# Expert matrices stored by partition, and the index of a job's rows loaded one job ahead

## The reference, cut to what matters

```python
N_EXPERTS = 32; TOP_K = 2; D_MODEL = 1024; EXPERT_HIDDEN = 512
order = jnp.argsort(flat_e)                     # flat_e: two experts per token
tok = order // TOP_K
xs = h[tok]
a = lax.ragged_dot(xs, w_gate, sizes)           # w_gate, w_up: (32, 1024, 512)
u = lax.ragged_dot(xs, w_up, sizes)
y = lax.ragged_dot(jax.nn.silu(a) * u, w_down, sizes)   # w_down: (32, 512, 1024)
y = y * w.reshape(-1)[order][:, None]
return jax.ops.segment_sum(y, tok, num_segments=n)
```

## Time and profile before

| | us |
|---|---|
| median of 3 runs | 4987.61 |
| profiled execution | 4986.04 |
| its span | 4984.5 |
| PE busy | 4524.7 (91% of the span) |
| DVE busy | 3301.9 (66%) |
| ACT busy | 2468.8 (50%) |
| POOL busy | 1185.4 (24%) |
| DMA mean | 218 GB/s over the span |

### The profile page before, as it was taken

One profiled execution on the slowest core, in us unless ns is written; L12 is line 12 of the kernel. 1 busy time (PEld: TensorE's weight loads), 2 busy tenths in 40 slices (PEclk: granted clock), 3 DMA queues, 4 the chain that ended last, 5 costly groups with the idle time before them and its releaser, 6 DMA issues. The chain is left out here.

```text
span 4984.5 us, 75902 instructions
## 1 busy us (share of the span) xinstructions
PE 4524.7 (91%) x25973; PEld 3778.5 (76%) x25973; DVE 3301.9 (66%) x5272; ACT 2468.8 (50%) x3056; POOL 1185.4 (24%) x919
## 2 busy tenths in 40 slices
PE   6999998899999897999957999999999987999995
PEld 4887877777878876777746878888877866877774
DVE  6653667676776568777777636677756437877776
ACT  3223555564233315777743225565633222777774
POOL 3650014400000012333334630053000001333333
PEclk8999999999999998999988999999999998999998
DMA  5645344264554567999995544253556345999998
GB/s 190 200 129 120 77 86 104 106 170 153 205 195 166 208 211 272 397 397 397 397 357 196 169 132 101 65 132 97 128 192 217 113 163 187 389 397 397 397 397 332
DMA packets 582022, 1088.92 MB, mean 218 GB/s; under 512 B 112100, under 2 KB 265604, under 8 KB 578776
## 3 DMA queue, kind: packets, MB, share of 16 engines
q1 hardware_dynamic: 532240, 919.40, 55.1%
q0 software_dynamic: 36208, 119.42, 6.4%
q10 hardware_dynamic: 13400, 47.85, 2.4%
HBM read 903.12 MB, written 183.43 MB: 218 GB/s over the span
## 5 line engine op out<-in xcount | busy, mean ns | idle before, releaser
L1817 PE MATMUL merge_acc<-ahead_wide,merge_w_split 128*128 128x512 f32 (+1 forms) x2880 | 640.9, 377 | 18.9 <-DMA ahead_wide<-hT 14.6
L1817 PEld LDWEIGHTS merge_acc<-ahead_wide,merge_w_split 128*128 128x128 f32 x2880 | 506.6, 191 | 126.9 <-issue 17.5
L665 PE MATMUL project_proj_acc<-ahead_wide,project_hT 128*128 128x512 f32 x2280 | 559.4, 397 | 3.1 <-DVE ahead_wide L486 2.0
L2534 DVE TENSOR_TENSOR experts_w_gate<-experts_raw_gate,experts_w_gate 128x2048 fp32r<-128x2048 f32 x146 | 363.1, 2493 | 300.6 <-ACT experts_w_gate L2456 300.6
L665 PEld LDWEIGHTS project_proj_acc<-ahead_wide,project_hT 128*128 128x128 f32 x2280 | 424.0, 190 | 93.3 <-DVE project_hT L516 4.5
L2436 POOL TENSOR_TENSOR experts_w_down<-experts_raw_down,experts_w_down 128x2048 fp32r<-128x2048 f32 x73 | 352.7, 4831 | 521.6 <-ACT experts_w_down L2456 521.6
L2580 PE MATMUL experts_gate_acc<-experts_w_gate,experts_rowsT 128*128 128x512 f32 x1752 | 423.7, 398 | 37.7 <-DVE experts_rowsT L2539 37.7
L981 DVE TENSOR_REDUCE attend_stat<-attend_scores 128x1 f32<-128x1280 f32 (+2 forms) x288 | 305.7, 1062 | 208.1 <-PE attend_scores L882 204.6
L2594 PE MATMUL experts_result_acc<-experts_w_down,experts_hiddenT 128*128 128x512 f32 x1752 | 423.5, 398 | 12.2 <-DVE experts_w_down L2534 12.2
L2580 PEld LDWEIGHTS experts_gate_acc<-experts_w_gate,experts_rowsT 128*128 128x128 f32 x1752 | 326.9, 190 | 119.7 <-issue 47.8
L2580 PE MATMUL experts_up_acc<-experts_w_up,experts_rowsT 128*128 128x512 f32 x1752 | 409.3, 389 | 0.0
(11 more groups left out here) (258 smaller groups left out, 8300.6 us busy)
## 6 DMA issues: line engine op xcount, KB each, us to landing
experts_raw_gate<-in_w_exp_gate_dram SPq DMA_DIRECT2D x146, 1024.0 KB, 13.9
experts_raw_up<-in_w_exp_up_dram SPq DMA_DIRECT2D x146, 1024.0 KB, 12.8
experts_raw_down<-in_w_exp_down_dram SPq DMA_DIRECT2D x146, 1024.0 KB, 11.5
ahead_rows<-in_w_merge_dram SPq DMA_DIRECT2D x120, 768.0 KB, 6.1
merge_mod_w_ada<-in_w_ada_rows_dram POOLq DMA_DIRECT2D x80, 512.0 KB, 3.6
qk<-project_staged SPq DMA_DIRECT2D x74, 512.0 KB, 3.2
ye<-ahead_rows ACTq DMA_DIRECT2D x73, 512.0 KB, 6.3
attend_keys<-qk SPq DMA_DIRECT2D x96, 320.0 KB, 5.6
```

The lines of the kernel that those rows point to most:

```text
L665: m = pe.matmul(acc[g % 2][:, :], hT[:, a, q * KP + k, t * P:(t + 1) * P], w_split[n % SLOTS][:, c, k, :], start=(q == 0 and i == 0 and k ...
L1817: m = pe.matmul(acc[:, b, 0:w], w_split[b][:, a, k, :], hT[:, x, k, 0:w], start=(i == 0 and k == 0), stop=(i == 2 and k == KD - 1))
L2534: dve.tensor_tensor(w[n][:, 1, half, :], raw[n][:, half, :], w[n][:, 0, half, :].bitcast(F32), ALU.subtract).then_inc(w_lo[n].sem, 1)
```

## The change

There are two parts.

1. The three expert matrices are laid out anew on the host, as other inputs of this kernel already are. Within a half, row k*128+p of the matrix now stands at place p*(rows/128)+k, so that everything that goes to partition p is one contiguous run of 8 KB. Before, partition p received 4 runs of 2 KB for gate and up (rows p, 128+p, 256+p, 384+p of 512 floats), and 2 runs of 4 KB for down. What arrives in SBUF is the same, byte for byte.

2. POOL's `gather` no longer loads the index. A new function `load_index(g)` does, and it is called one job ahead: the loop runs `gather(g+2)`, `load_index(g+3)`, `rest_of_down(g)`, where it ran index load, gather, `rest_of_down`. The last gather leaves the loop, which is one round shorter.

```diff
     rows = w.shape[2] // 2
-    return w[l, e, half * rows:(half + 1) * rows, :].rearrange("o (k p) n -> p (o k) n", p=P)
+    return w[l, e, half * rows:(half + 1) * rows, :].rearrange("o (p k) n -> p (o k n)", p=P)
...
+            def load_index(g):
+                if later(g, 1):
+                    pool.wait_ge(x_in.sem, x_in.done(g - 1))
+                if isinstance(g, int):
+                    start = g * T
+                else:
+                    start = pool.value_load(starts[0:1, ds(g, 1)], min_val=0, max_val=NE * T - P)
+                pool.dma_start(index[:, :], scr["token_of"][ds(start, P), :]).then_inc(i_in.sem, 16)
+
             def gather(g):
                 if isinstance(g, int) and g == 0:
                     pool.wait_ge(d.index_in.sem, d.index_in.done(0))
                 else:
-                    pool.wait_ge(x_in.sem, x_in.done(g - 1))
-                    if isinstance(g, int):
-                        start = g * T
-                    else:
-                        start = pool.value_load(starts[0:1, ds(g, 1)], min_val=0, max_val=NE * T - P)
-                    pool.dma_start(index[:, :], scr["token_of"][ds(start, P), :]).then_inc(i_in.sem, 16)
                     pool.wait_ge(i_in.sem, i_in.done(g - 1))
+                if later(g, 1):
                     pool.wait_ge(xt.sem, xt.done(g - 1))
...
             gather(0)
+            load_index(1)
             gather(1)
             n_jobs = load_count(pool)
+            load_index(2)
             gather(2)
+            load_index(3)
             rest_of_down(0)
-            with pool.Fori(1, n_jobs - 2) as g:
+            with pool.Fori(1, n_jobs - 3) as g:
                 gather(g + 2)
+                load_index(g + 3)
                 rest_of_down(g)
+            gather(n_jobs - 1)
+            rest_of_down(n_jobs - 3)
             rest_of_down(n_jobs - 2)
             rest_of_down(n_jobs - 1)
...
+        halves = w.reshape(DEPTH, NE, 2, rows // (2 * P), P, n).transpose(0, 1, 2, 4, 3, 5)
+        return np.ascontiguousarray(halves).reshape(DEPTH, NE, rows, n)
```

More of the change, by code:

```diff
@@ L2710, in laid_out, with by_partition @@
     two = 2 * KD
-    return {"w_ada_rows0": np.concatenate([w_ada[0][two:], w_ada[1][:two]]), "w_ada_rows1": w_ada[1][two:],
+    def by_partition(name):
+        w = np.asarray(inputs[name])
+        rows, n = w.shape[2:]
+        halves = w.reshape(DEPTH, NE, 2, rows // (2 * P), P, n).transpose(0, 1, 2, 4, 3, 5)
+        return np.ascontiguousarray(halves).reshape(DEPTH, NE, rows, n)
+    return {"w_exp_gate": by_partition("w_exp_gate"), "w_exp_up": by_partition("w_exp_up"),
+            "w_exp_down": by_partition("w_exp_down"),
+            "w_ada_rows0": np.concatenate([w_ada[0][two:], w_ada[1][:two]]), "w_ada_rows1": w_ada[1][two:],
             "b_ada_columns0": np.concatenate([b_ada[0][two:], b_ada[1][:two]]).T, "b_ada_columns1": b_ada[1][two:].T,
```

## The result

The changed kernel is slower. Median of 11 runs 5032.48 us (4998.86 to 5066.94), beside 4987.61 us for the kernel before in its 11 runs on the same chip (4979.27 to 4992.7). The ratio is 1.0095, with a 95% interval of 1.0074 to 1.0116. The forecast was 4947.5 us with a range to 4972: a gain was forecast and a loss came. The profiled execution took 5038.14 us with a span of 5036.5, which is 52.0 more than before.

The account below looks back on a forecast made before the run. Transfers were taken to bound the expert jobs at 18.50 us, PE next at 17.76. Saving 44.9 us and losing 4.8 at the layer starts gave -40.1, so 4947.5 us; own range 4940 to 4955, wider range 4940 to 4972.

Parts of the forecast that it names:

- The bound: Expert jobs: transfers set 18.50 us a job, with PE close behind at 17.76 us.
- Part 1, the rate: Expert matrix loads: 8 KB runs move at 425 GB/s, transfers need 17.45 us, PE sets 17.76; saving 44.9 us.
- Rival A: Expert jobs: the rate stays at 397 GB/s and a job at 18.50 us; about 4990 us, chance 0.10 with D.
- Part 2, the landing L: Gather on POOL, issue to landing: 8.6 us taken, bounds 7.0 and 12; low part of down not held below 10.7.
- Part 2, the loop: Gather, index load, low part, DVE, PE over two jobs: a job takes 12.4 + L/2; forecast to cost nothing.
- B: Expert jobs: gather late in part, or rate in between; a job about 18.1 us, about 4972 us, chance 0.15.
- C: Expert jobs: gather landing above 12.2 us makes jobs slower than 18.50; 5023 to 5057 us, chance 0.05.
- Part 2, the start: Each layer's first jobs: first low part of down starts 2.3 and 2.5 us later; 4.8 us lost in all.
- The removed wait: POOL, between index load and gather: about 5.2 us of wait removed, which PE does not feel; costed at nothing.
- D: Expert matrix loads: runs cut to 2 KB again, so nothing moves but the start; counted in A's 0.10.

Follow-up runs that it names:

- second index tile: Changed kernel, but the next index is loaded into a tile of its own and copied by POOL ahead of the gather, without waiting for a landing: 4940.99 us, ratio 0.9901.
- runs of 4 KB: Changed kernel with all three expert matrices in runs of 4 KB, index still loaded a job ahead: 4951.02 us, ratio 0.992.

## Why the prediction was wrong

**The bound (right).** 18.50 us a job by transfers and 17.76 by PE were the two limits. The second index tile shows both: PE busy without a gap from 2030 to 2420, 533.16 us for the 30 jobs (1990.93 to 2524.09), 17.77 each.

**Part 1, the rate (right where it can show).** 413 GB/s and a saving of 21.6 + 22.6 = 44.2 us in the kernel with the second tile, against 44.9 forecast. The 425 GB/s and 17.45 us of the sum can't be seen, since PE sets the pace there. Rival A is out. The 358 GB/s for transfers between HBM and SBUF that the prediction took from the Trainium skill (DMA: Bandwidth & Descriptors, "Where 436 GB/s comes from") don't bind on this one core: it moved 397 GB/s before and 413 now. At 4 KB the transfers by the prediction's own sum need 6.291/0.411 + 2.65 = 17.96 us, and jobs took 17.73 to 17.98.

**Part 2, the landing L (wrong; this is the step that failed).** "I take 8.6, nearer to the rows of 6 KB. Then the loop pays nothing, with 2 us to spare." The term L was mis-sized: measured 12.1 us (2060 to 2300), 12.4 (4350 to 4600) and 11.2 (4580 to 4905) where the kernel is slow, around the upper bound of 12, and 9.5 (2330 to 2550) where it is fast. What the sum put at nothing in the loop, the index load's wait for the landing ahead of the low part of down, set the pace of most jobs. Two things make L. One is the packets: 7.0 to 10.5 us with the old POOL code. The other is that the gather, issued some 5 us earlier in the job, falls beside DVE's gate halves, where the issue alone takes up to 2.5 us and not 0.97; by the index order alone L was 9.0 in place of 7.0. The prediction placed the gather at 4292.9 and DVE's gate halves from 4289.18 to 4296.63 in the same job, and kept the L of the old place. Both together, with jobs on time, gave 10.93 us from issue to index load at 2355.44.

The room itself was also too wide. The prediction let 0.7 us pass from the landing to the end of the index load. In the loop the gather of 2088.78 landed after 11.7 us and its index load began after 12.97, that of 2355.44 after 9.5 and 10.93; with 0.57 for the load this is 1.9 to 2.0 us. The order rows show why: the load of the job's first row number (`TENSOR_LOAD experts_starts`) now stands behind the wait for the landing. So of the 11.45 us from 4292.9 to 4304.35 only about 9.5 are left for L, and not 10.7, and the 9.5 of the fast way just fits. The remaining 1.7 to 2.9 us of L come when POOL is late. A likely reason is this: SP's load of the second half of down waits for the low part, and the next pair of gate loads is then issued close behind it and just beside the gather. The SP rows of the changed kernel:

```profile
2088.47 0.33 SPq L2397 DMA_DIRECT2D experts_raw_down<-in_w_exp_down_dram  x1
2090.11 1.04 SPq L2397 DMA_DIRECT2D experts_raw_gate<-in_w_exp_gate_dram  x2
```

The gather was issued at 2088.78, between a load of down and two of gate. That lateness so feeds on itself would explain why the kernel ran most jobs from 2325 to 2556 at 17.77 us and others at 19; this is argued from the rows, and no experiment shows it alone. What starts and ends the slow way stays open.

**Part 2, the loop (wrong in form).** The prediction halved a chain of two jobs through DVE and PE, 12.4 + L/2. The one that closed lies on POOL alone, is one job long, and moves by a full us for each us of landing: S + 6.1. S is L and 1.3 to 1.4 more. The two let a job of 17.76 pass up to nearly the same L, 10.7 and 10.3, but above it they part: the 11.7 of the job shown gives 18.25 us by the halved one, and the ring took 19.08. So B's middle of 4972 was set too low, and C's door too far off.

**Part 2, the start (mechanism right, sizes off).** The low part of job 0 starts at 1945.99 in layer 0, where 1942.5 was forecast and 1940.19 was before, and at 4274.85 in layer 1. Against the first gather of its layer that is 4.9 and 7.2 us later than before, where 2.3 and 2.5 were forecast: the landing of the gather of job 1 holds up the index load and the gather of job 2 too, which the sum left out. The second job of the layer took 1.5 us longer in layer 0 (19.91 against 18.36) and 3.3 in layer 1 (21.06 against 17.77), 4.8 together, as forecast, which is luck; and the jobs behind it did not recover, and the starts as a whole cost 5.1 + 12.4 = 17.5 us. (The sum's lower bound at L = 7.0 comes out at 1.6 us by its own rows, not 1.4.)

**The removed wait (right about its worth, wrong about what is free).** The index load a job ahead was worth nothing: 0.9994 by itself with the short runs. What was not seen is that a single index tile ties gather, landing and next index load into a ring in either order. With 8 KB packets it closes at 19.28 us with the old order and at 19.08 with the new one, in the jobs shown.

**The rivals.** C is what happened: "POOL's index load waiting for the gather's landing and the low part of down behind it", at 18.8 to 19.2 us a job. It was priced at 5023 to 5057 us, which holds the measured 5032.48, and given 0.05. That the price fits is luck in part: it took L = 13 to 14 in the halved form and put 11 to 15 us on the start. At the measured L of 12.1 that form gives B's 18.45 us, less than before. A chance of 0.05 needed L to be known, and the one row beside it was for packets of another size on another transfer. D is out: from 2060 to 2300 the same stretch has 14676 packets, where it had 38628.

## What to carry to other kernels

Before making the packets of a full queue longer, list the transfers of other queues on whose landing something waits, follow each ring through their buffers, and ask how much longer a landing it bears; longer packets gained 4% in rate here and lengthened the gather's landing by half. When an index or a list is loaded a job ahead, give it a tile of its own: loading earlier into a single tile only moves the wait. Where an issue moves within the job, look at what it will then run beside, and do not carry its old duration over. Where the gain of long runs is wanted with less risk, half of their length gave most of the gain here (0.9915 against 0.9901).

## What the runs showed of the hardware that was not expected

- Landing of a gather of 128 rows of 4 KB beside the loads of the matrices: 7.0, 7.9 to 8.4 and 10.3 to 10.8 us with runs of 2 to 4, 4 and 8 KB in these, POOL's code being that of before; the store of a job's result, 512 KB too, 6.3, 7.0 to 7.5 and 8.1 to 8.7 us; the index load of 0.5 KB 4.9, 4.9 and 5.2 to 6.2 us.
- Issuing the gather takes POOL 0.97 us in the quiet and 2.2 to 2.5 beside DVE's gate halves, and a copy of 128x1 on POOL takes 2.25 us there, but 0.18 where no DVE instruction of this kind runs beside it (the first copy of a layer). The plain index load takes POOL 0.56 to 0.60 us to issue in either place. Of the engines' side the Trainium skill (SBUF — State Buffer, "Who interferes with whom") says that a DVE operation with two inputs in SBUF contends with a GpSimd instruction that reads SBUF. The low halves are such operations, the copy reads SBUF, and the rows agree. In the second tile's kernel DVE's two gate halves run from 2087.96 to 2095.67; the copy lies within them, the issue of the gather in part. That the gather's issue is slow because it reads its index from SBUF is not shown.

```profile
1928.52 0.18 POOL L2430 COPY experts_index<-experts_index_next 128x1 int32<-128x1 int32 x1 [8.82 <-DMA experts_index_next<-token_of]
```

- A time set by landings spreads: the changed kernel's 11 runs lie 68 us apart, the 12 of the layout alone 48. With either cure it goes: 5 us in the second index tile's 4 runs, 6 in the 5 runs of 4 KB.
- A stop of PE of 1.9 to 2.6 us was followed by a granted clock of 0.50 to 0.65 for 3 to 4 us in four cases, and by none in another of 2.62 us.
